# Norms between layers: one root and one reciprocal per token, with tokens on partitions, spread again by a diagonal and a matmul by ones

## The reference, cut to what matters

```python
def _rmsnorm(x, g):
    xf = x.astype(f32)
    y = xf * lax.rsqrt(jnp.mean(xf * xf, axis=-1, keepdims=True) + NORM_EPS)
    return (y * g).astype(x.dtype)

def _sublayer(x, c, w_ada, b_ada, g_pre, g_post, fn):
    mod = (jax.nn.silu(c) @ w_ada + b_ada)[:, None, :]
    shift, scale, gate = jnp.split(mod, 3, axis=-1)
    h = _rmsnorm(x, g_pre) * (1 + scale) + shift
    y, aux = fn(h)
    return x + gate * _rmsnorm(y, g_post), aux
```

## Time and profile before

| | us |
|---|---|
| median of 3 runs | 2562.42 |
| lowest, highest | 2557.11, 2563.34 |
| the profiled execution: its device time | 2554.93 |
| its span, first to last instruction | 2553.2 |
| its mean granted TensorE clock | 0.927 |

### The profile page before, as it was taken

One profiled execution on the slowest core, in us unless ns is written; L12 is line 12 of the kernel. 1 busy time (PEld: TensorE's weight loads), 2 busy tenths in 40 slices (PEclk: granted clock), 3 DMA queues, 4 the chain that ended last, 5 costly groups with the idle time before them and its releaser, 6 DMA issues. The chain is left out here.

```text
span 2553.2 us, 63593 instructions
## 1 busy us (share of the span) xinstructions
PE 2238.4 (88%) x26373; PEld 1738.9 (68%) x26373; DVE 1419.1 (56%) x2304; ACT 872.6 (34%) x1619; POOL 383.5 (15%) x434
## 2 busy tenths in 40 slices
PE   6798899989768987799999979998888876999998
PEld 3565777777538864577777757664777764777776
DVE  2436777877574547654422265557777757553234
ACT  2326544444322222333322131146434323332222
POOL 2003133333100000111100000015233310110000
PEclk8899999999869977899999989999898898999999
DMA  7413899999750034123223324450999921332331
GB/s 245 116 50 103 289 329 343 342 329 338 248 173 11 4 120 127 54 75 89 85 83 92 91 67 140 133 181 28 311 320 327 306 67 37 88 90 83 92 88 58
DMA packets 308011, 392.68 MB, mean 154 GB/s; under 512 B 25025, under 2 KB 226059, under 8 KB 307749
## 3 DMA queue, kind: packets, MB, share of 16 engines
q1 hardware_dynamic: 278036, 282.66, 35.6%
q0 software_dynamic: 29712, 106.25, 12.1%
HBM read 378.15 MB, written 10.70 MB: 152 GB/s over the span
## 5 line engine op out<-in xcount | busy, mean ns | idle before, releaser
L851 PE MATMUL bank<-yT,WH 128*128 128x288 f16 x3200 | 533.2, 290 | 45.8 <-DVE yT L705 34.6
L851 PEld LDWEIGHTS bank<-yT,WH 128*128 128x128 f16 x3200 | 314.7, 99 | 145.1 <-issue 48.8
L915 DVE SCALAR_TENSOR_TENSOR WL<-wring,WH 128x1024 f16<-128x1024 f32 x180 | 238.3, 1328 | 255.6 <-ACT WH L895 255.4
L1411 DVE TENSOR_TENSOR KL<-bank,KH 128x512 f16<-128x512 f32 x416 | 277.7, 686 | 135.1 <-ACT KH L1389 71.8
L1389 ACT CAST KH<-bank 128x512 f16<-128x512 f32 x416 | 237.3, 585 | 335.6 <-PE bank L1304 316.7
L851 PE MATMUL bank<-uT,WH 128*128 128x288 f16 x2048 | 337.9, 288 | 10.6 <-DVE WL L915 10.6
L851 PE MATMUL bank<-yT,WL 128*128 128x288 f16 x1600 | 332.3, 290 | 0.0
L895 ACT ACTIVATE WH<-wring 128x1024 f16<-128x1024 f32 x180 | 189.0, 1054 | 253.2 <-PE bank L851 221.1
L851 PEld LDWEIGHTS bank<-uT,WH 128*128 128x128 f16 x2048 | 201.5, 98 | 63.3 <-DVE WL L915 11.2
L851 PE MATMUL bank<-uT,WL 128*128 128x288 f16 x1024 | 210.8, 288 | 0.0
L851 PEld LDWEIGHTS bank<-yT,WL 128*128 128x128 f16 x1600 | 158.6, 99 | 42.0
(11 more groups left out here) (473 smaller groups left out, 4165.6 us busy)
## 6 DMA issues: line engine op xcount, KB each, us to landing
wring<-in_ada_w SPq DMA_DIRECT2D x96, 512.0 KB
vTd<-in_state_dil_k SPq DMA_DIRECT2D x160, 256.0 KB
yT<-in_cache_fox_k SPq DMA_DIRECT2D x128, 256.0 KB
krows<-in_cache_fox_k SPq DMA_DIRECT2D x128, 256.0 KB
wring<-in_mlp_up SPq DMA_DIRECT2D x64, 512.0 KB
wring<-in_mlp_down SPq DMA_DIRECT2D x64, 512.0 KB
wring<-in_ev_w_in SPq DMA_DIRECT2D x26, 512.0 KB
wring<-in_od_w_in SPq DMA_DIRECT2D x24, 512.0 KB
```

The lines of the kernel that those rows point to most:

```text
L851: last = nc.tensor.matmul(bank[b + h][:, 0:HALF], w[s % 2][:, c, :], x[:, s % parts * KC + c, h * HALF:(h + 1) * HALF], start=(s % parts = ...
L915: nc.vector.scalar_tensor_tensor(WL[s % 2][:, :, :], w[:, :, :], WSCALE, WH[s % 2][:, :, :], ALU.mult, ALU.subtract).then_inc(w_free, 1)
L1411: nc.vector.tensor_tensor(KL[i][:, :], turned[n % NT][:, :], KH[i][:, :], ALU.subtract).then_inc(lo_out, 1)
```

## The change

The norms between sub-layers, and the last one, are computed in another layout. `token_sums` takes the squares as weights, 128 tokens at a time, and moves a single column of ones through them: the sums of 128 tokens come out on 128 partitions, one column for each of 5 groups of tokens (the fifth group begins at token 448, so that its upper 64 partitions are the samples). One root and one reciprocal of 128 x 5 follow. `token_inverse` then multiplies the identity by these numbers, giving four diagonal blocks of 128 x 128 and one of 64 x 64 in `std`, and `spread_inverse` multiplies them by the matrix of ones on PE, which puts the reciprocals on all partitions again: 512 columns in one bank, 64 in another. The products that used `rstd` in SBUF now read these banks in PSUM; in `add_chunks` the 64 sample columns of all 8 chunks are multiplied by one instruction ahead of the loop, and the loop handles 512 columns. A root of one column is added at the end of every gated projection, on ACT (`after_act`, tile `warm`).

```diff
+    def token_sums(pe, out, src, first, final):
+        for t in range(NTILE + 1):
+            lo = min(t * P, TOK - P)
+            last = nc.tensor.matmul(out[:, t:t + 1], src[:, lo:lo + P], C["ones"][:, 0:1], start=(first and t == 0), stop=final, skip_group_check=True)
+        return last
+
+    def token_roots(act, sums, done):
+        nc.scalar.activation(root5[:, :], sums[:, 0:NTILE + 1], ACT.Sqrt, bias=eps_rms, scale=1.0 / D).then_inc(done, 1)
+
+    def token_inverse(dve, root_ok, inv_ok, diag_ok):
+        dve.wait_ge(root_ok, 1)
+        nc.vector.reciprocal(inv5[:, :], root5[:, :]).then_inc(inv_ok, 1)
+        dve.wait_ge(inv_ok, 1)
+        nc.vector.tensor_tensor(std[:, 0:NPR].rearrange("p (t q) -> p t q", q=P), ident.unsqueeze(1).to_broadcast([P, NTILE, P]),
+                                inv5[:, 0:NTILE].unsqueeze(2).to_broadcast([P, NTILE, P]), ALU.mult).then_inc(diag_ok, 1)
+        nc.vector.tensor_scalar(std[NDEC:P, NPR:TOK], ident[NDEC:P, NDEC:P], inv5[NDEC:P, NTILE:NTILE + 1], None, ALU.mult).then_inc(diag_ok, 1)
+
+    def spread_inverse(pe, sums, out, diag_ok, spread_ok):
+        pe.wait_ge(diag_ok, 2)
+        nc.tensor.matmul(sums[:, NDEC:2 * NDEC], C["ones"][NDEC:P, :], std[NDEC:P, NPR:TOK], start=True, stop=True)
+        nc.tensor.matmul(out[:, :], C["ones"], std[:, 0:NPR], start=True, stop=True).then_inc(spread_ok, 1)
+
     def add_chunks(dve, scaled, added):
+        late = slice(NPR, TOK)
+        nc.vector.tensor_tensor(yT[:, :, late], yT[:, :, late], bank[4][:, NDEC:2 * NDEC].unsqueeze(1).to_broadcast([P, KC, NDEC]), ALU.mult).then_inc(scaled, 1)
         for k in range(KC + 1):
             if k < KC:
-                nc.vector.tensor_tensor(yT[:, k, :], yT[:, k, :], rstd[:, :], ALU.mult).then_inc(scaled, 1)
+                nc.vector.tensor_tensor(yT[:, k, 0:NPR], yT[:, k, 0:NPR], bank[5][:, :], ALU.mult).then_inc(scaled, 1)
             if k:
-                dve.wait_ge(scaled, k)
+                dve.wait_ge(scaled, k + 1)
                 nc.vector.tensor_tensor(xT[:, k - 1, :], xT[:, k - 1, :], yT[:, k - 1, :], ALU.add).then_inc(added, 1)
...
         def on_pe(pe):
+            if add:
+                spread_inverse(pe, bank[4], bank[5], diag1, spread1)
             for k in range(KC):
                 pe.wait_ge(squared, k + 1)
-                last = ones_sums(pe, bank[6:8], hT[:, k, :], k == 0, k == KC - 1)
+                last = token_sums(pe, bank[6], hT[:, k, :], k == 0, k == KC - 1)
             last.then_inc(sum2, 1)
+            spread_inverse(pe, bank[6], bank[7], diag2, spread2)
...
         def on_act(act, splits):
             if add:
-                roots(act, bank[4:6], std1)
+                token_roots(act, bank[4], std1)
...
-                roots(act, bank[6:8], std2)
+                token_roots(act, bank[6], std2)
...
         def on_dve(dve, splits):
             if add:
-                inverse(dve, std1, inv1)
+                token_inverse(dve, std1, inv1, diag1)
+                dve.wait_ge(spread1, 1)
                 add_chunks(dve, scaled, added)
...
             if not root_known:
-                inverse(dve, std2, inv2)
+                token_inverse(dve, std2, inv2, diag2)
+                dve.wait_ge(spread2, 1)
...
         def after_pe(pe):
             pe.wait_ge(acc_ok, KC)
-            ones_sums(pe, bank[4:6], acc, True, False)
+            token_sums(pe, bank[4], acc, True, False)
             pe.wait_ge(sq_a, KC)
             pe.wait_ge(sq_d, 2 * KC)
-            ones_sums(pe, bank[4:6], sq, False, True)
+            token_sums(pe, bank[4], sq, False, True)
+
+        def after_act(act):
+            nc.scalar.activation(warm[:, :], eps_rms, ACT.Sqrt)
```

More of the change, by code:

```diff
@@ L218, in build_trunk @@
     scT = sb(top, "scT", [P, KC, 32])
+    root5, inv5 = sb(top, "root5", [P, NTILE + 1]), sb(top, "inv5", [P, NTILE + 1])
+    warm = sb(top, "warm", [P, 1])
     pt_sb = sb(top, "pt_sb", [1, NSEQ * PAGES], I32)
@@ L648, in renorm @@
         smp, high_s, rest_s, u_ok, high_ok, rest_ok, whole_ok = (sem(n) for n in ("smp", "high_s", "rest_s", "u_ok", "high_ok", "rest_ok", "whole_ok"))
+        diag1, spread1, diag2, spread2 = (sem(n) for n in ("diag1", "spread1", "diag2", "spread2"))
         B, A = 24 * sub, 24 * sub + 8
@@ L652, in renorm @@
         of_seq = lambda j: mod[:, j:j + KC, 1:9].unsqueeze(3).to_broadcast([P, KC, NSEQ, NNEW])
+        inv_prompt, inv_late = (rstd[:, 0:NPR], rstd[:, late]) if root_known else (bank[7][:, :], bank[6][:, NDEC:2 * NDEC])
         def on_pe(pe):
@@ L671, in on_act @@
                 act.wait_ge(sum2, 1)
-                roots(act, bank[6:8], std2)
+                if add:
+                    act.wait_ge(inv1, 1)
+                token_roots(act, bank[6], std2)
             act.wait_ge(smp, 3)
@@ L695, in on_dve @@
             if not root_known:
-                inverse(dve, std2, inv2)
+                token_inverse(dve, std2, inv2, diag2)
+                dve.wait_ge(spread2, 1)
             dve.wait_ge(smp, 1)
-            nc.vector.tensor_tensor(hT[:, :, late], yT[:, :, late], rstd[:, late].unsqueeze(1).to_broadcast([P, KC, NDEC]), ALU.mult).then_inc(smp, 1)
+            nc.vector.tensor_tensor(hT[:, :, late], yT[:, :, late], inv_late.unsqueeze(1).to_broadcast([P, KC, NDEC]), ALU.mult).then_inc(smp, 1)
             def unit(k):
-                nc.vector.scalar_tensor_tensor(hT[:, k, 0:NPR], xT[:, k, 0:NPR], mod[:, A + k, 0:1], rstd[:, 0:NPR], ALU.mult, ALU.mult).then_inc(u_ok, 1)
+                nc.vector.scalar_tensor_tensor(hT[:, k, 0:NPR], xT[:, k, 0:NPR], mod[:, A + k, 0:1], inv_prompt, ALU.mult, ALU.mult).then_inc(u_ok, 1)
             def remainder(k):
@@ L779, in after_pe @@
             pe.wait_ge(acc_ok, KC)
-            ones_sums(pe, bank[4:6], acc, True, False)
+            token_sums(pe, bank[4], acc, True, False)
             pe.wait_ge(sq_a, KC)
             pe.wait_ge(sq_d, 2 * KC)
-            ones_sums(pe, bank[4:6], sq, False, True)
+            token_sums(pe, bank[4], sq, False, True)
+        def after_act(act):
+            nc.scalar.activation(warm[:, :], eps_rms, ACT.Sqrt)
         def after_dve(dve):
             dve.wait_ge(smp_d, KC)
-        project_split(k, rhs, copy_act, copy_dve, after_pe=after_pe, after_dve=after_dve, on_pool=on_pool, before=before, unrolled=True,
+        project_split(k, rhs, copy_act, copy_dve, after_pe=after_pe, after_act=after_act, after_dve=after_dve, on_pool=on_pool, before=before, unrolled=True,
                       sp_last=sp_last)
@@ L2723, in add_and_store @@
         std1, inv1, scaled, added, turned, row_a, smp_a = (sem(n) for n in ("std1", "inv1", "scaled", "added", "turned", "row_a", "smp_a"))
+        diag1, spread1 = sem("diag1"), sem("spread1")
         with ExitStack() as sc:
```

## The result

| | before | after |
|---|---|---|
| median of 10 runs each, us | 2561.81 | 2585.96 |
| lowest, highest, us | 2551.02, 2566.46 | 2571.42, 2597.52 |
| span of the profiled execution, us | 2553.2 | 2584.5 |
| its mean granted TensorE clock | 0.927 | 0.912 |

After to before is 1.0100, with a 95% interval of 1.0083 to 1.0116. Of the 2561.81 us of before that is 25.6 us more, 21.3 to 29.7. The forecast was 16.8 us more, and 2579 us with a range of 2558 to 2589. The time lies in the range, and the sign, the place and the mechanism came out as forecast; the size is 9 us larger.

What follows compares the result with a forecast made beforehand. PE paces the whole, but at the norms a chain over four engines does. Passages of + 6.3, + 6.2 and + 4.6 us and - 0.3 at the end make + 16.8 on 2562.4: 2579 us, range 2558 to 2589.

Steps and rivals of the forecast that it cites:

- Leg C: PE's sums of the new squares over 8 chunks until the second roots: 17.2 us at 1.2 GHz, against 10.56.
- rival one: Weight loads count as work and the clock returns during the sums, or loads are not slowed: 2559 us; chance 14%.
- rival two: The clock never falls, as the spread splits PE's idle time in two: - 12.9 us, 2549.5 us; chance 5%.
- Legs A and D: First roots to first product, and second roots to the samples' product: 3.9 us each at 1.2 GHz, against 4.33.
- The spread: Matmuls on PE putting the reciprocals back on all partitions, within A and D: 2.5 us at 1.2 GHz, 1.25 at 2.4.
- Leg B: First product for the add to the first sum of new squares on PE: 3.3 us, against 2.86.
- The sums at the block's end: Sums of the output's squares at the gated projection's end: + 0.1 us where 1.21 stood, still at full clock.
- the table load: Third passage, ahead of its roots: the extra root moves it beside the sums, - 1.28 us, at worst - 1.0.
- The end of the program: The last norm, with only leg A and the adds: - 0.3 us.
- the three passages: Full chains of two norms between projections, legs A to D: + 6.3, + 6.2 and + 4.6 us.
- Rival three: Early sums also at 1.2 GHz (+ 0.9, four times), next projection longer at 0.50 (+ 1.5, three times): 2587 us; chance 9%.

Runs made afterwards that it cites:

- after_double: The changed kernel with every chunk's narrow sums made twice, the second set unused: 1.0295 of the kernel before, + 75.4 us.
- after_busy: The changed kernel with unused 288-column float32 matmuls in PE's idle time around the two spreads, none among the narrow sums: 1.0044 of before, + 11.2 us.
- after_again: The changed kernel once more, unchanged, for its trace: one run, span 2580.9 us.
- second_only: The kernel before with the new layout only for the norm of the new x, no early root: 1.0126 of before, + 32 us.
- f16_squares: The changed kernel with the squares of the new x and their column of ones in float16: 1.0013 of before, + 3.3 us.
- f16_early: As f16_squares, with DVE's two weight splits moved to its wait for the first spread: 0.9997 of before, - 0.8 us.
- f16_early_busy: As f16_early, with the extra wide matmuls of after_busy: 0.9942 of before, - 14.8 us.
- f16_held: As f16_early_busy, with one more wide matmul behind the sums of each of the first seven chunks: 0.9957 of before, - 11.0 us.
- before_again: The kernel before once more, unchanged, for its trace: one run, span 2555.0 us.

## Why the prediction was right, and where its size was off

**Leg C: right, to 0.1 us.** Forecast 80 x 0.213 + 0.2 = 17.2 at 1.2 GHz, measured 17.26, 17.23 in each passage for the PE row. Of the three ways in which it could have gone, rival one (the loads bring the clock back) and rival two (it never falls) are out: 0.50 in every window of the sums, the same slow pace for 34 us in after_double, and a fall in the midst of such work in after_busy. Against the earlier trace rows C is + 6.7, + 6.6 and + 6.2.

By the Trainium skill ("TensorE: Matmul & The Clock Gate", LDWEIGHTS), as weighed in the prediction, a load of 128 columns is 107 ns; the 17.14 us of PEld for 80 loads here are 214 ns each, at 1.2 GHz. The measurement decides.

**Legs A and D: 4.3 in place of 3.9.** (Only A of the second passage was 3.92, its spread partly at full clock.) Two terms were mis-sized. The spread is 1055.82 + 2.07 - 1055.20 = 2.69 us where 2.5 at 1.2 GHz were forecast, as the 64-column matmul takes 0.62 until the wide one starts (0.43 forecast). The rest, DVE and the handovers, is 1.60 against 1.37, of which the fifth block is 0.26 instead of 0.08 (0.18) and the reciprocal 0.19 instead of 0.16. Five of the six inverses thus save 0.04 us, not 0.43, which is 1.9 us of the missing 9.

**Leg B: 3.32, forecast 3.3.** A product that reads PSUM costs what it costs from SBUF: 0.69 for 512 columns (L664, L737), as L698 did in the earlier trace rows.

**The rest of the forecast's sum.** The sums at the block's end take 1.25 (forecast 1.3, the clock still up), and the table load is hidden as forecast. The end of the program, from root to end, is 20.3 and 19.8 against 20.3 and 20.4: - 0.3 forecast, - 0.3 measured as a mean of the two.

By rows, then, the three passages are + 7.1, + 6.6 and + 6.6 less the hidden load of 1.3: + 18.9 from the unrounded marks. With the end, + 18.6.

**Rival three's second half came in part.** The next projection stays at 0.50 for 5.6 us where the earlier trace rows had 3, as that rival said; at the second passage it is 3.3 and at the third 5.2. But the stretch from the samples' product of the first passage to the next roots, 397.46 before, is 396.84 after and 396.78 in after_again. The + 1.5 is not there, because before pays elsewhere. At the gap of 3.11 us some 16 us on, before lost its clock and after kept it. Windows behind the gap, in before:

```profile
1098.00:1100.00 2.00, 1.82 (x9) 1.26 (x10) 1.66 (x4) 0.96 (x2) 0.73 (x1) 0.60 0.24 52
1100.00:1102.00 2.00, 2.00 (x11) 1.27 (x10) 1.55 (x2) 0.00 (x0) 0.00 (x0) 0.55 0.73 214
```

and in after:

```profile
1106.00:1108.00 2.00, 2.00 (x18) 1.60 (x17) 1.82 (x3) 0.00 (x0) 0.00 (x0) 1.00 0.82 235
```

Behind the third passage both lost it at that gap, and there the stretch is 398.93 against 397.69, + 1.2 (in after_again 397.76, + 0.1, with 3.7 us of the projection at 0.50). Before, then after:

```profile
2158.00:2160.00 2.00, 2.00 (x10) 1.29 (x9) 1.44 (x2) 0.00 (x0) 0.00 (x0) 0.52 0.75 223
```

```profile
2188.00:2190.00 2.00, 2.00 (x11) 1.25 (x10) 1.70 (x4) 0.00 (x0) 0.00 (x0) 0.56 0.74 215
```

**What stays open.** 25.6 us are measured (21.3 at the least) and 18.6 explained by rows. The rest is 3 to 11 us, most of the 9 by which the forecast was short. It isn't the variation between the runs, which the interval contains. By their times, kernels with narrow sums in leg C have such a rest too: some 13 us in second_only and 6 in f16_squares and f16_early. But in f16_early_busy and f16_held, which have them as well, passages, table load and MLP stretches account for the time.

The rows don't place it. The three kernels with the wide sums there and no filling have a "rest" of 2486.3, 2489.0 and 2490.1, the three with one dose of narrow float32 sums 2497.4, 2494.3 and 2496.3, the two with float16 sums 2494.2 and 2494.0. Of the 7.5 us between the first two means 5.3 lie in the second mixer's stretch, in which one kernel alone varies by 8.7, and 1.3 in the stretch after the third passage. And after_double, with twice the narrow sums, has 2488.1, as little as before. The stretch ahead of the first roots alone, in which the kernels hardly differ, runs from 1043.7 us (f16_early_busy) to 1055.4 (before).

So it is not shown that the rest belongs to the narrow sums. If it does, it is no price per matmul, as far as the 11 us of uncertainty in after_double's second dose can say. A shift of when the second mixer begins against its transfers, the clock's state on entering it, or something outside both: no run here tells them apart.

## What to carry to other kernels

Swapping the operands of a sum by ones (data as weights, one column moving) saved nothing on TensorE here, where the data are float32: 40 matmuls took 17.2 us where 16 of 288 columns took 10.5, as each of their 80 records has a weight load of its own (PEld busy for 17.14 us) and none of them keeps the clock up. In float16 the same 40 were hidden behind their supply. Before a costly vector operation is replaced by a short one plus a spread through PE, price the spread at 1.2 GHz if PE has been idle around it: here it took back all but 0.04 us of the gain, at each of five places. And when PE idles on a chain that can't be shortened, filling it with wide matmuls can be worth more than the shortening: - 5.9 us for the untouched kernel, and - 14.8 with float16 squares and early splits, which alone gave - 0.8.

## What the runs showed of the hardware

- A PE that the profile shows busy all the time, on matmul and weight load both, may be at half clock and stay there, 34 us long in after_double. A clock that is up falls under such work (0.94 to 0.50 at 1062 in after_busy). In the passages only work with 288 columns was followed by its return.
- The same gap of 3.1 us in the projection costs the clock in one execution and not in another. After the first passage it fell in six of the table's thirteen profiles (before, before_again, second_only, f16_squares, f16_early, f16_held) and not in the other seven, although second_only has the legs C and D of after. It costs about 1.6 us, by one less the clock over the windows behind the gap (in before 0.40 x 1.82 + 0.45 x 2.00).
- A reciprocal on DVE took 3.77 us for two of 288 columns and 0.19 for one of 5.
